# Splitting two output-projection weight tiles ahead of their ring slots in a fused encoder on Trainium2

## What is computed

```python
o_a = block_attention(q_a, k_a, v_a)            # 8 query heads, 2 key/value heads
o_b = block_attention(q_full, k_full, v_b)      # 8 heads from low-rank latents
o = concatenate([rms_norm(o_a, g_out_a), rms_norm(o_b, g_out_b)], -1) @ w_o
x = x + gate_a * o
h = rms_norm(x, g_ffn) * (1.0 + scale_f) + shift_f
u = depthwise_conv_centred(h @ w_up, conv_w, conv_b)
val, gate = split(u, 2, -1)
x = x + gate_f * ((silu(gate) * val) @ w_down)  # D_FF = 2816
```

## Time and profile before

| | |
|---|---|
| median of 3 runs | 1166.56 us (1166.42 to 1166.7) |
| profiled execution | 1166.48 us, of which span 1164.7 us |
| TensorE busy, matmuls | 1130.2 us (97% of the span) |
| VectorE busy | 740.1 us (64%) |
| GpSimd busy | 590.1 us (51%) |
| ScalarE busy | 513.9 us (44%) |
| GpSimd's subtractions (line 589) | 712 of mean 803 ns |
| ScalarE's casts (line 1232) | 178 of mean 1047 ns |

### The profile page before, as it was taken

The page is one execution under the profiler, slowest core; times in us unless marked ns, Lnnn a source line. Parts: engine busy times, 40 slices in busy tenths (PEclk is TensorE's granted clock), DMA queues, the critical chain, the costliest instruction groups (busy, mean ns, idle before and its releaser), DMA issues.

```text
span 1164.7 us, 18672 instructions
## 1 busy us (share of the span) xinstructions
PE 1130.2 (97%) x6252; PEld 938.5 (81%) x6252; DVE 740.1 (64%) x1434; ACT 513.9 (44%) x936; POOL 590.1 (51%) x783
## 2 busy tenths in 40 slices
PE   7999999899999999999999889999999999999996
PEld 4796678798888888888889857799888888888886
DVE  3398676767766778768679887746775144413445
ACT  4736774354422443134444477545443244323442
POOL 2563343655554554655658514255555555555652
PEclk8999999999999999999999999999999999999999
DMA  9744611324455343644333411022433323223222
GB/s 372 287 163 145 224 50 33 132 73 170 156 182 197 126 178 143 220 161 150 141 109 119 154 55 37 20 76 88 163 126 99 100 90 101 97 91 107 92 72 73
DMA packets 43687, 150.60 MB, mean 129 GB/s; under 512 B 5089, under 2 KB 7905, under 8 KB 43489
## 3 DMA queue, kind: packets, MB, share of 16 engines
q1 hardware_dynamic: 43184, 149.61, 36.9%
q10 hardware_dynamic: 432, 0.10, 0.0%
HBM read 147.59 MB, written 2.10 MB: 129 GB/s over the span
## 4 chain that ended last, share of the span: by engine, by line
issue 46%; POOL 36%; POOLq 16%; PE 1%; DVE 0%; DVEq 0%; ACT 0%
POOL w_lo L589 35%; POOLq L591 12%; POOLq L649 2%; POOLq L647 1%; POOLq L602 0%; PE ps L676 0%; POOLq L587 0%; PE ps L682 0%; PE ps L677 0%; DVE x L1667 0%; POOLq L592 0%; POOL cg_sg L620 0%; POOL cg_sg L622 0%; PE ps L696 0%; PE ps L688 0%
## 5 line engine op out<-in xcount | busy, mean ns | idle before, releaser
L589 POOL TENSOR_TENSOR w_lo<-w_raw,w_hi 128x256 fp32r<-128x256 f32 x712 | 550.0, 803 | 454.4 <-ACT w_hi L1232 435.8
L676 PE MATMUL ps<-h_hi,w_hi 128*128 128x512 f32 (+1 forms) x864 | 316.4, 366 | 2.0 <-POOLq L592 1.7
L677 PE MATMUL ps<-h_lo,w_hi 128*128 128x512 f32 (+1 forms) x864 | 315.7, 365 | 0.0
L682 PE MATMUL ps<-h_hi,w_lo 128*128 128x512 f32 (+1 forms) x864 | 315.7, 365 | 0.0
L1232 ACT CAST w_hi<-w_raw 128x1024 fp32r<-128x1024 f32 x178 | 185.8, 1047 | 191.9 <-PE ps L676 189.8
L2004 DVE SCALAR_TENSOR_TENSOR u_sb<-ps,par,u_sb 128x510 f32<-128x510 f32 x176 | 131.8, 749 | 111.6 <-ACT u_sb L1459 98.0
L676 PEld LDWEIGHTS ps<-h_hi,w_hi 128*128 128x128 f32 x864 | 162.9, 189 | 28.6 <-POOLq L592 2.7
L682 PEld LDWEIGHTS ps<-h_hi,w_lo 128*128 128x128 f32 x864 | 162.9, 189 | 26.4
L677 PEld LDWEIGHTS ps<-h_lo,w_hi 128*128 128x128 f32 x864 | 162.9, 189 | 26.1
L676 PE MATMUL ps<-a_hi,w_hi 128*128 128x512 f32 (+1 forms) x400 | 146.0, 365 | 1.3 <-POOLq L592 1.1
L682 PE MATMUL ps<-a_hi,w_lo 128*128 128x512 f32 (+1 forms) x400 | 145.4, 364 | 0.0
(11 more groups left out here) (186 smaller groups left out, 1451.2 us busy)
## 6 DMA issues: line engine op xcount, KB each, us to landing
w_raw<-w_slots SPq DMA_DIRECT2D x178, 512.0 KB, 3.5
ada_raw<-ada_slots SPq DMA_DIRECT2D x88, 512.0 KB, 4.3
first_raw<-first_slots SPq DMA_DIRECT2D x8, 512.0 KB, 13.1
x<-x_t SPq DMA_DIRECT2D x4, 512.0 KB, 6.0
y_t<-x SPq DMA_DIRECT2D x3, 512.0 KB, 3.0
c_all<-c_wide SPq DMA_DIRECT2D x1, 1024.0 KB, 17.0
y_t<-x SPq DMA_DIRECT2D x1, 256.0 KB, 3.0
y_t<-x SPq DMA_DIRECT2D x2, 128.0 KB, 2.7
```

The lines of the kernel that those rows point to most:

```text
L589: nc.gpsimd.tensor_tensor(w_lo[:, j, c], w_raw[:, j, c], w_hi[:, j, c].bitcast(F32), ALU.subtract)
L676: hh = mm(out, stat[0], mov[0], start=first, stop=False)
L677: hl = mm(out, stat[0], mov[1], start=False, stop=False)
L682: return mm(out, stat[1], mov[0], start=False, stop=last)
```

## The change

The `hi` and `lo` parts of the output projection's tiles 4 and 5 (slots 17 and 18 of a layer, `S_SPARE` = S_WO + RING) are no longer put in the ring, but in two spare places, `spare_hi` over `prob` and `spare_lo` over `prob_t`. `parts_of(n)` gives the place of a slot's parts. ScalarE casts the two behind the casts of the attention outputs 4 to 7, without asking `slot_free`. GpSimd subtracts for them before its loop, after waiting for the last attention output.

The ring places which these two slots would have had stay empty, so the first two up slots are cast earlier (`early_hi`): ahead of squares 4 and 5. The casts of tiles 6 and 7 stay ahead of squares 2 and 3. ScalarE's `norm` now gets a list: in the norm of this stage it casts only the third and the fourth up slot, where the second and the fourth were cast. The norm at a layer's end casts as before.

```diff
+SPARE = 2
+S_SPARE = S_WO + RING
...
+        spare_hi = put("spare_hi", [P, SPARE, SLOT], F32R, at=at_att)
+        spare_lo = put("spare_lo", [P, SPARE, SLOT], F32R, at=at_att + 8192)
...
+        def parts_of(n):
+            e = n % SLOTS - S_SPARE
+            if 0 <= e < SPARE:
+                return spare_hi[:, e, :], spare_lo[:, e, :]
+            return w_hi[:, n % RING, :], w_lo[:, n % RING, :]
...
+            def lo_spare(n):
+                hi, lo = parts_of(n)
+                pool.wait_ge(hi_done, n + 1)
+                for q in range(4):
+                    c = slice(q * SLOT // 4, (q + 1) * SLOT // 4)
+                    nc.gpsimd.tensor_tensor(lo[:, c], w_raw[:, n % RING, c], hi[:, c].bitcast(F32), ALU.subtract)
+                nc.gpsimd.drain()
+                pool.sem_inc(raw_free, 1)
+                pool.sem_inc(split_done, 1)
...
-                lo_slots(L * SLOTS + S_WO + 4, L * SLOTS + SLOTS)
+                pool.wait_ge(o_done, NP * (L + 1))
+                for n in range(L * SLOTS + S_SPARE, L * SLOTS + S_SPARE + SPARE):
+                    lo_spare(n)
+                lo_slots(L * SLOTS + S_SPARE + SPARE, L * SLOTS + SLOTS)
...
-                j = slot(L, S_WO + m)
+                slot(L, S_WO + m)
+                w = parts_of(L * SLOTS + S_WO + m)
...
-                    last = product(ps[:, bank(key), c], [r[:, j, k * P:k * P + P] for r in (w_hi, w_lo)],
+                    last = product(ps[:, bank(key), c], [r[:, k * P:k * P + P] for r in w],
...
-            def norm(n, L, s_next):
+            def norm(n, L, slots):
+                def next_hi(i):
+                    if slots[i] is not None:
+                        split_hi(L, slots[i])
...
+            def spare_cast(L, e):
+                n = L * SLOTS + S_SPARE + e
+                act.wait_ge(raw_landed[n % RING], 16 * (n // RING + 1))
+                nc.scalar.copy(parts_of(n)[0], w_raw[:, n % RING, :]).then_inc(hi_done, 1)
+
+            def early_hi(L, s):
+                n = L * SLOTS + s
+                act.wait_ge(slot_free, n + 1 - RING)
+                act.wait_ge(raw_landed[n % RING], 16 * (n // RING + 1))
+                nc.scalar.copy(w_hi[:, n % RING, :], w_raw[:, n % RING, :]).then_inc(hi_done, 1)
...
+                for e in range(SPARE):
+                    spare_cast(L, e)
                 group_roots(L, 2)
...
                 for e in range(N_UPD - 4):
-                    if e < TAIL:
-                        split_hi(L, S_WO + 4 + e)
+                    if TAIL - SPARE <= e < TAIL:
+                        split_hi(L, S_WO + RING + e)
+                    elif TAIL <= e < TAIL + SPARE:
+                        early_hi(L, S_UP[0] + e - TAIL)
                     square(2 * L + 1, e)
-                norm(2 * L + 1, L, S_WO + KD)
+                norm(2 * L + 1, L, (None, S_UP[0] + 2, None, S_UP[0] + 3))
```

More of the change, by code:

```diff
@@ L1200, in square @@
                 A(sq_x[:, e % 2, c], x[:, m, c], ACT.Square).then_inc(sq_ready, 1)
-            def norm(n, L, s_next):
+            def norm(n, L, slots):
+                def next_hi(i):
+                    if slots[i] is not None:
+                        split_hi(L, slots[i])
                 root_of_norm(n, 0)
                 square(n, N_UPD - 4)
-                split_hi(L, s_next)
+                next_hi(0)
                 square(n, N_UPD - 3)
@@ L1214, in norm @@
                 make_h(n, 0, 0, 2)
-                split_hi(L, s_next + 1)
+                next_hi(1)
                 make_h(n, 0, 2, 3)
@@ L1218, in norm @@
                 make_h(n, 0, 3, 4)
-                split_hi(L, s_next + 2)
+                next_hi(2)
                 make_h(n, 0, 4, 5)
@@ L1222, in norm @@
                 make_h(n, 0, 5, 6)
-                split_hi(L, s_next + 3)
+                next_hi(3)
                 make_h(n, 0, 6, KD)
@@ L1481, in _ @@
                             square(2 * L + 2, e)
-                        norm(2 * L + 2, L, S_DOWN[g] + KD)
+                        norm(2 * L + 2, L, [SLOTS + e for e in range(RING)])
         @block.vector
```

## The result

| | kernel before | changed kernel |
|---|---|---|
| median | 1166.94 us (1166.42 to 1168.74, 10 runs) | 1170.24 us (1168.19 to 1173.29, 10 runs) |
| profiled execution | 1166.48 us | 1169.98 us |

The ratio is 1.0026, with a 95% interval of 1.0017 to 1.0034: the changed kernel is 3.3 us slower, where the forecast was +1.1 us and the range ended at 1169.3.

What follows compares the result with a forecast made beforehand. TensorE was taken as busy almost throughout, with VectorE the gate of layer 0's norm sums. -4.0 + 4.2 + 1.3 - 0.4 = +1.1 on 1166.48 gave 1167.6 us; own range 1166.6 to 1168.6, wider range 1165.2 to 1169.3.

Steps and rivals of the forecast that it cites:

- What bounds the kernel: TensorE works almost throughout, with 5.7 us of gaps; in layer 0 VectorE sets when the norm's sums can start.
- (a): Output projection, layer 0: tiles 4 and 5 split early, TensorE's stalls of 2.40 and 1.60 us go: -4.0 us.
- (b): Norm's sums, layer 0: VectorE takes the 4 us back as one wait, plus 0.2 for meetings with GpSimd: +4.2 us.
- (c): Half tile behind layer 0's norm sums: the one long gap lowers TensorE's clock: +1.3 us, between 0 and 3.4.
- a long low stretch: Rival: the half tile behind layer 0's norm sums runs wholly at half speed, +2.9; total +2.7, 1169.2 us; chance 0.20.
- (d): First up tile, both layers: stalls of 0.86 and 0.87 us go, 1.3 of 1.73 come back as waits: -0.4 us.
- (e): The rest, casts of up slots 0 and 1 and two written-out slots of GpSimd's loop: costs nothing.
- the slow rival: Same as a long low stretch: +0.2 + 2.9 - 0.4 = +2.7 us, 1169.2 us; chance 0.20.

Runs made afterwards that it cites:

- thin products: Modulation products in layer 0's output-projection norm cut from 1024 to 64 columns, in the kernel before and in the changed kernel: 1161.94 and 1162.06 us.
- The chain without the late meetings: Changed kernel with the casts of the first two up slots put back in the norm, spare places kept: 1169.09 us, 28.59 us to the sums.
- layer 0 alone: Kernel before with the change made in layer 0 only, layer 1 as before: 1170.95 us, ratio 1.0027.
- late sums: Changed kernel with TensorE's norm sums in layer 0 behind the second half tile of sequence 1 instead of the first: 1168.03 us, ratio 1.0007.
- fill the gap: Changed kernel with 20 constant matmuls on TensorE ahead of layer 0's norm sums: 1168.09 us, ratio 1.0008.
- layer 1 alone: Kernel before with the change made in layer 1 only, layer 0 as before: 1167.29 us, ratio 1.0004.
- the one without spare slots: Kernel before with up slots 0 and 1 cast as a pair, the next two at third and fourth place, and late sums: 1169.75 us, ratio 1.0018.
- the fastest version: Changed kernel with up slots 0 and 1 cast as a pair behind the first square, the next two one position later, and late sums: 1165.42 us.

## Why the prediction was wrong

- **What bounds the kernel**: right. The stalls for GpSimd lay in VectorE's shadow; the thin products show it.
- **(a)**, -4.0 on TensorE: right in kind, a little small. The wait of 5.68 us at the sums is not the 4.0 + 0.26 alone: VectorE came 0.86 us later, and the stall of 0.4 us foreseen at tile 7 isn't in the waits table (4.0 + 0.26 + 0.86 = 5.1). The other 0.6 lie at the starts of tiles 5, 6 and 7, about 0.2 each: their first matmul takes 0.39 us in the kernel before and 0.28 here, and the second starts 0.22 us behind it and 0.12 here, which no wait counts. The eight subtractions for the spare slots were hidden.
- **(b)**, the gate: **the first step that failed.** The mechanism was named and its bound of +1.3 held, but I took +0.2 "since they stand in the last, thinning part", and +0.86 was measured. Operation by operation, the two traces give a net -0.7 where GpSimd no longer meets VectorE early, and +1.5 from five operations that it meets later (0.36 and 0.21 on an add and a product near 210 us, then 0.33, 0.31 and 0.30 on the three rows above): the count, -0.6 and +1.3 to +1.9, was about right, and the discount to +0.2 was the mistake, since GpSimd's part was not thinning and ran to 219.3. The chain without the late meetings, 28.59, shows that the early casts cost 2.14 us, against a relief of 1.28 by the spare slots. The rule of the Trainium skill (SBUF — State Buffer, the section on two separate sides), which would have given +3.6, is farther off still: single operations lost 0.30 to 0.54 us against their time alone (the product of 1.77 us the most), and none of those shown here a whole subtraction's 0.71.
- **(c)**, the clock: **the second and larger one.** I took +1.3, between 0 and a stretch of 3.4 us, and had the long stretch as a rival with +2.9. In the changed kernel's two profiles and in that of layer 0 alone the gap was 5.68 us and the stretch behind it 6.8 to 7 us: +1.77, +2.40 and +2.40 from the sums to the update. The likeliest case was thus the rival "a long low stretch", with a price between my two. The mechanism, one gap, a low clock behind it and the half tile that VectorE waits for, was right; the term was mis-sized, +1.3 for +1.8 to +2.4. Why the same gap and stretch cost two prices shows in how much of the stretch ran out while TensorE still waited (the first profile of the changed kernel, then the second; the sums start at 221.76 and 222.86):

```profile
218.00:222.00 4.00, 0.24 (x2) 0.24 (x2) 3.03 (x9) 0.42 (x1) 1.24 (x1) 0.61 0.56 175
...
219.00:223.00 4.00, 0.14 (x1) 0.14 (x1) 3.03 (x9) 0.42 (x1) 1.34 (x1) 0.81 0.54 168
```

(1 - 0.61) x 8 - 0.24 = 2.9 us of it in the one and (1 - 0.81) x 8 - 0.14 = 1.4 us in the other. What I set against the rival, a clock that stayed up after 2.40 us, was the reading of one execution; the second profile of the same kernel shows it falling. By the Trainium skill (TensorE: Matmul & The Clock Gate, the HAM clock gate) the low level is the default, and activity lifts it. For the long gaps the traces agree: all five waits of 3.65 us and more at these sums were followed by it. For short ones they don't decide: 2.40 us were followed by it in one profile of four.
- **(d)**, the head of the up projection: inside its bounds. -0.33 in layer 1 and +0.26 in layer 0, where a gain of 0.2 was forecast, together -0.1 for -0.4; the stall for GpSimd became one for VectorE's second sums (0.97 and 0.42 us), as said.
- **(e)**: nothing was seen there.

By the measured terms the sum is 0.86 + 1.77 to 2.40 + 0.26 - 0.33 = +2.6 to +3.2 us, that is 1169.0 to 1169.7 from the profiled 1166.48, and the measured ratio gives +3.0. The kernel before also had a median of 1166.94 this time, 0.4 us above the 1166.56 of the forecast; that is part of the distance to 1170.24, and no part of the mechanism. The range ended at 1169.3 because the slow rival in it (+2.7) paired the high clock cost with the low value of (b): two terms with a common cause, GpSimd's work being moved late, were taken as if their bad ends excluded each other.

## What to carry to other kernels

If an engine's stalls lie in the shadow of another one, removing them moves them to where it waits for that one, as one long gap; ask what the engine does right behind that point and at what clock, and give it independent work to put in front of it (late sums: 2.2 us) or fill the gap (2.1 us). Work that is moved earlier on one engine can land beside the last part of the gate, where it has no slack: count the meetings one by one on both sides, and don't discount the count (here -0.7 and +1.5 were measured, +0.2 taken). Of the orders tried, the edit was worth its buffers only together with the order of two other steps (1165.42 us), and either part alone was slower than the kernel before.

## What was not expected of the hardware

TensorE's clock doesn't answer to the length of a gap alone. A gap of 2.40 us in layer 0 was followed by no low stretch in three profiles (before, layer 1 alone, the one without spare slots) and by 3.4 us at 1.2 GHz in one; 2.50 us by 3.4; 3.65 us by 7.0 in one kernel, and 3.66 us by 3.4 in another; 5.68 us by about 7 in all three. Shorter waits show it too: 0.76 and 0.55 us close together were followed by 3.4 us in the fastest version, and 1.23 us behind the 20 matmuls by none. The cost on the path ranged from nothing to 2.6 us. One profile can't show which it will be, so a cost of this kind is a range.

GpSimd's subtraction of 256 columns takes 706 ns alone, 821 and 784 beside VectorE with thin products and 1138 to 1196 beside full ones, so in this kernel a lighter VectorE beside it is what made GpSimd fast.
